# Attention scores from three terms instead of four, the low-part products of two heads in separate row halves of TensorE

## The chip, the cores and the metric

The kernel runs on one core of one Trainium2 chip. The metric is the device time of one execution in microseconds (us), the median of three runs. Engines are named as in the profile: PE is TensorE's matrix products, PEld its weight loads, DVE is VectorE, ACT is ScalarE, POOL is GpSimd, SPq is the queue of SyncE, which issues all DMAs.

## The reference

One residual block over 2048 rows of width 1024, float32. After an RMS norm, one projection gives q, k, v and the gates. Attention has four pairs of heads; each pair has two heads of 64 features for q and k, and one value head of 128 features. What matters here is one tile of 128 queries against the keys it may see:

```
sc = jnp.einsum('bqhd,bkhd->bhqk', qb, k) * scale        # two heads (h) of a pair, d = 64
sc = jnp.where(mask, sc, jnp.finfo(jnp.float32).min)     # chunk-causal
pr = jax.nn.softmax(sc, axis=-1).reshape(b, ATT_HEADS, 2, Q_BLOCK, s)
a  = pr[:, :, 0] - lam * pr[:, :, 1]
out = jnp.einsum('bhqk,bkhe->bqhe', a, v)
```

The rest (a short gated convolution, gates by sigmoid, two output projections, a norm) stands before and behind the attention.

## The kernel before

Float32 values are split in a high part of type fp32r and a low part, the rest. A product of two matrices is then a sum of products of parts: high by high, high by low, low by high (`split_product`, L936 to L939).

The stages in order: the norm and the v projection; the other projections (28 tiles of 128 features by 4 blocks of 512 rows, L973 to L980), whose q and k parts go to `qk_s` in memory; the attention stage; then for each block of 512 rows the two branch projections and `w_out`.

The attention stage has rounds R, one per tile of 128 queries (4 pairs by 16 tiles), laid out by the class `Plan`. In round R, PE computes the scores of tile R+1 (`score`, L987), turns the combined probabilities of tile R-1 with the identity (`turn`, L1003), and in every second round multiplies two tiles by the values (`values`, L1014). Keys come in chunks of up to 512. The positions are causal, so a tile has 1 to 4 chunks, its last one 128, 256, 384 or 512 wide. In all there are 160 chunks: 112 of 512 columns and 16 of each of the other three widths. Between these steps PE does the gate projections (`gates`, L1051, products at L1065), 1536 products of 512 columns that depend on nothing in the attention and fill its waits. `Plan` divides them over the rounds by comparing `tensor_columns` and `vector_columns`.

A chunk's scores are four products, two for each head. The key tile `k_sl` holds for each head the high part in partitions 0 to 63 and the low part in 64 to 127. The query tile `q_st` holds the same query part twice, in both halves of the partitions. So one product with 128 rows gives q_high by (k_high + k_low) (L999), and the other q_low by (k_high + k_low) (L1000): four terms in two products. The result lies in one of three banks, `bank[0]`, `bank[1]`, `bank[4]`, taken in turn. DVE then adds the mask, copies the scores to `e1` or `e2` and takes the maximum (`mask_max`, L1580, semaphore `scored`). A head's first product waits until the bank's last user is scored, three products back. After the last chunk DVE forms the bias (L1587, L1589), ACT the exponentials (L1267), DVE combines both heads (L1600), PE turns the result (L1010), ACT copies the high part (L1276), DVE the low part (L1616), and PE multiplies by the values (L1027).

SyncE issues `load_q` (L678, four DMAs for two tiles of queries), `load_k` (L662, two DMAs for 512 keys), `load_v` (L669), the gate weights `load_unit` (L685) and the stores, in one order.

Of the kernel before, what the change touches and what calls it, by code (L numbers as in the profile page):

```python
# [14 lines left out]
P = 128  # L15
# [58 lines left out]
UNITS = GATE_TILES * NB  # L74
PER_UNIT = 3 * KT
LEAD = 2 * PER_UNIT
K_IN, V_IN, Q_IN = 2 * 16, 2 * 16, 4 * 16
RING = 5

WO_AT = ((), (), (0,), (1,), (2,), (3,), (4, 5), (6, 7))  # L80
# [66 lines left out]
class Plan:  # L147
# [64 lines left out]
    def tensor_columns(self, R):  # L212
        n = 0
        if 0 <= R + 1 < TILES:
            n += 4 * self.keys(R + 1)
        if 0 <= R - 1 < TILES:
            n += 2 * self.keys(R - 1)
        if R % 2 == 0 and 2 <= R <= TILES:
            n += 6 * max(self.keys(R - 1), self.keys(R - 2))
        return n + 1200  # L220
# [32 lines left out]
def build(nc, t):  # L253

    with ExitStack() as whole:
# [3 lines left out]
        def held(name, shape, dt=F32, ctx=whole):  # L259
            return ctx.enter_context(nc.sbuf_tensor(name, shape, dt))  # L260
# [77 lines left out]


        kc = held("kc", [P, S], F32, room)  # L340
        q_st = [held(f"q_st{b}", [P, 2, 2, QB], F32R, room) for b in range(2)]
        k_sl = {i: held(f"k_sl{i}", [P, 2, BLK], F32R, room) for i in (3, 0, 1, 2)}
        sub = ExitStack()
        first_w = [held(f"first_w{i}", [P, 2, KT, P], F32R, sub) for i in range(2)]
# [191 lines left out]
        def _(sp):  # L536
# [121 lines left out]

            def load_k(plan, pair, c):
                i = plan.slot(pair * NT, c)  # L660
                for half in range(2):
                    sp.dma_start(k_sl[i][half * HD:(half + 1) * HD].bitcast(F32),  # L662
                                 qk_s[1, half, pair * P:(pair + 1) * P, c:c + BLK].rearrange("(h j) n -> j h n", h=2)
                                 ).then_inc(k_loaded[i], 16)

            def load_v(plan, pair, c):
                i = plan.slot(pair * NT, c)
# [5 lines left out]
            def load_q(plan, B):  # L673
                pair, ti = plan.tile(2 * B)
                qs = slice(ti // 2 * QB, ti // 2 * QB + QB)
                for half in range(2):
                    for at in (0, HD):
                        sp.dma_start(q_st[B % 2][at:at + HD, half].bitcast(F32),  # L678
                                     qk_s[0, half, pair * P:(pair + 1) * P, qs].rearrange("(h j) n -> j h n", h=2)
                                     ).then_inc(q_loaded[B % 2], 16)  # L680

            def load_unit(u):
                if u >= 4:
# [251 lines left out]
        def _(pe):  # L935
# [48 lines left out]
            score_bank = (0, 1, 4)  # L984

            def attend(plan):
                def score(G, c, wide, h):  # L987
                    ti = plan.tile(G)[1]
                    if h == 0 and plan.first_use(G, c):
                        pe.wait_ge(k_loaded[plan.slot(G, c)], (G // NT + 1) * K_IN)  # L990
                    if G % 2 == 0 and c == 0 and h == 0:
                        pe.wait_ge(q_loaded[G // 2 % 2], (G // 4 + 1) * Q_IN)
                    o = 2 * (plan.before(G) + c // BLK) + h
                    if o >= 3:
                        pe.wait_ge(scored, o - 2)
                    out = bank[score_bank[o % 3]][:, 0:wide]
                    k = k_sl[plan.slot(G, c)][:, h, 0:wide]
                    qs = slice(ti % 2 * P, ti % 2 * P + P)
                    nc.tensor.matmul(out, q_st[G // 2 % 2][:, 0, h, qs], k, start=True, stop=False)  # L999
                    nc.tensor.matmul(out, q_st[G // 2 % 2][:, 1, h, qs], k, start=False, stop=True  # L1000
                                     ).then_inc(qk_done, 1)

                def turn(G, c, wide):  # L1003
                    if c == 0:
                        pe.wait_ge(combined, G + 1)
                    o = plan.before(G) + c // BLK
                    if o >= 2:
                        pe.wait_ge(at_lo_done, o - 1)
                    for k in range(wide // P):
                        mm = nc.tensor.transpose(bank[5 + o % 2][:, k * P:(k + 1) * P],  # L1010
                                                 e1[G % 2][:, c + k * P:c + (k + 1) * P], ident[:])
                    mm.then_inc(turned, 1)

                def values(G, c, wide):  # L1014

                    B = G // 2
                    last = max(plan.keys(G - 1), plan.keys(G)) // P - 1
                    pe.wait_ge(at_lo_done, plan.before(G) + c // BLK + 1)
                    if plan.first_use(G, c) or plan.first_use(G - 1, c):
                        pe.wait_ge(v_loaded[plan.slot(G, c)], (G // NT + 1) * V_IN)  # L1020
                    if c == 0 and B:
                        pe.wait_ge(o_normed, B)

                    def step(k, x, start, stop):
                        q0 = P if plan.causal and k == last else 0
                        v = v_sl[plan.slot(G, k * P // BLK * BLK)][:, x // 2, k % QPB, :]
                        return nc.tensor.matmul(bank[7][:, q0:QB], v, (at_lo if x == 1 else at_hi)[:, k, q0:QB],  # L1027
                                                start=start, stop=stop)

                    if c == 0:  # L1030
                        step(0, 0, True, False)
                    for k in range(max(c // P, 1), (c + wide) // P):
                        for x in range(3):
                            step(k, x, False, False)
                    if (c + wide) // P - 1 == last:
                        step(0, 1, False, False)
                        step(0, 2, False, True).then_inc(pv_done, 1)

                def square_sums(B):
                    pe.wait_ge(sq_done, B + 1)  # L1040
                    if B:
                        pe.wait_ge(ln_done, B)
                    pe.wait_ge(es_ready, 2 * (B + 1))
                    nc.tensor.matmul(bank[7][:, QB:2 * QB], ones[:], o_sq[:], start=True, stop=False)
                    for i in range(2):
                        q0 = QB + plan.tile(2 * B + i)[1] % 2 * P
                        mm = nc.tensor.matmul(bank[7][:, q0:q0 + P], es[(2 * B + i) % 4][:], ident[:],
                                              start=False, stop=i == 1)
                    mm.then_inc(ss_done, 1)

                def gates(part):  # L1051
                    for x in range(part[0], part[1]):
                        u, i = divmod(x, PER_UNIT)
                        k, term = divmod(i, 3)
                        bb, g = divmod(u, GATE_TILES)
                        if i == 0:
                            if u < 2:
                                pe.wait_ge(first_in[u], 16)
                            else:
                                pe.wait_ge(unit_w[u % 2], 16 * (u // 2))  # L1060
                            if u >= 2:
                                pe.wait_ge(gate_out, u - 1)
                        if bb and g == 0 and term == 0 and k % 2 == 0:
                            pe.wait_ge(ht_in[k // 2], 32 * bb)
                        mm = nc.tensor.matmul(bank[2 + u % 2][:], unit_weights(u)[:, term // 2, k, :],  # L1065
                                              h_slot(bb, k)[:, term % 2, :], start=i == 0, stop=i == PER_UNIT - 1)
                        if i == PER_UNIT - 1:
                            mm.then_inc(unit_done, 1)
                        elif g == GATE_TILES - 1 and i == 5 and bb < NB - 1:
                            mm.then_inc(ht_free, 1)  # L1070


                pe.wait_ge(dve_done, done_at(LINE - 2, 3))
                gates((0, LEAD))
                pe.wait_ge(dve_done, done_at(LINE - 1, 0))
                for R in plan.rounds:
                    steps = plan.round(R)
                    for j, (turned_part, scored_part, value_part, part) in enumerate(steps):
                        if turned_part:
                            turn(R - 1, *turned_part)  # L1080
                        if scored_part:
                            for h in range(2):
                                score(R + 1, *scored_part, h)
                        if value_part:
                            values(R - 1, *value_part)
                        if R % 2 == 1 and 3 <= R <= TILES + 1 and j == min(1, len(steps) - 1):
                            square_sums((R - 3) // 2)
                        gates(part)
# [663 lines left out]
```

## Time and profile before

| | us |
|---|---|
| median of three runs | 1808.36 (1807.6 to 1809.15) |
| the profiled execution, its own time | 1808.52 |
| its span in the profile | 1806.7 |
| PE busy | 1758.4 (97%) |
| PEld busy | 1466.7 (81%) |
| DVE busy | 893.8 (49%) |
| ACT busy | 580.3 (32%) |
| DMA, mean rate | 182 GB/s |

Some 1.8 us lie outside the span. A product of 512 columns is shown as 390 ns long, but the next one starts about 227 ns after it: the shown length holds the time in the pipeline, so PE's busy share is a mark of where PE has work, and the distance from start to start is the cost of a product. Weight loads lie under the product before them. A row of the timeline gives start, length, engine, line, operation, tiles, sizes and how many instructions were merged, and in brackets idle time that the engine spent before it and what ended it.

### The profile page before, as it was taken

To read this page: it belongs to the slowest core of one execution; us is meant where nothing else is said; L and a number is where in the kernel's file an instruction comes from. 1 tells how busy PE (TensorE), PEld (TensorE's weight loads), DVE (VectorE), ACT (ScalarE), POOL (GpSimd) and SP (SyncE) were. 2 spreads that over 40 slices of the span, in tenths; PEclk is the share of its full clock that TensorE was granted. 3 is DMA by queue.
4 is the path that set the end of the run, shared out by engine and by line. 5 is a ranking of instruction groups with operands and counts; after the bars stand their busy time and mean duration, and the time that the engine had idled before them with its cause. 6 is when DMAs were issued, how large, how long until landed. Compare 5 with 4: busy or idle time off the path is not lost.

```text
span 1806.7 us, 22424 instructions
## 1 busy us (share of the span) xinstructions
PE 1758.4 (97%) x8512; PEld 1466.7 (81%) x8512; DVE 893.8 (49%) x1903; ACT 580.3 (32%) x1039; POOL 89.0 (5%) x74
## 2 busy tenths in 40 slices
PE   7999999999999999999999999999899889999998
PEld 6887888888888888788887888888788768888887
DVE  5547244445334511276666666766576344424242
ACT  5423112121101111245444544444444333313231
POOL 0000000000000000111101111111001000000000
PEclk9999999999999999999999999999999999999999
DMA  6557346465503546965674778556856775453532
GB/s 233 164 189 314 129 163 210 163 210 167 178 18 129 162 118 174 265 219 186 198 211 151 221 233 271 181 180 208 248 158 185 227 281 172 120 181 111 175 105 76
DMA packets 149574, 328.90 MB, mean 182 GB/s; under 512 B 14801, under 2 KB 68049, under 8 KB 135889
## 3 DMA queue, kind: packets, MB, share of 16 engines
q1 hardware_dynamic: 149458, 327.37, 57.3%
q8 instruction: 70, 1.15, 0.3%
q14 instruction: 46, 0.38, 0.1%
HBM read 216.16 MB, written 111.16 MB: 181 GB/s over the span
## 4 chain that ended last, share of the span: by engine, by line
PE 83%; DMA 7%; ACT 3%; SPq 3%; DVE 2%; issue 2%; DVEq 0%; ACTq 0%
PE bank L937 18%; PE bank L938 18%; PE bank L939 18%; PE bank L1065 15%; PE bank L1027 5%; PE bank L999 3%; PE bank L1000 3%; PE bank L1010 2%; DMA raw<-in_w_in 2%; DMA ring<-gate_s 2%; SPq L669 2%; ACT e L1267 2%; DMA w<-split_s 1%; DMA gate_s<-gate_st 1%; DVE at_lo L1616 1%
## 5 line engine op out<-in xcount | busy, mean ns | idle before, releaser
L937 PE MATMUL bank<-ht,w 128*128 128x512 f32 x896 | 349.9, 390 | 3.0 <-issue 3.0
L938 PE MATMUL bank<-ht,w 128*128 128x512 f32 x896 | 349.7, 390 | 0.0
L939 PE MATMUL bank<-ht,w 128*128 128x512 f32 x896 | 349.5, 390 | 0.0
L1065 PE MATMUL bank<-ht,w 128*128 128x512 f32 x912 | 238.8, 396 | 4.0 <-DMA w<-split_s 4.0
L937 PEld LDWEIGHTS bank<-ht,w 128*128 128x128 f32 x896 | 168.8, 188 | 38.7 <-issue 3.4
L939 PEld LDWEIGHTS bank<-ht,w 128*128 128x128 f32 x896 | 168.9, 188 | 35.2
L938 PEld LDWEIGHTS bank<-ht,w 128*128 128x128 f32 x896 | 168.9, 188 | 35.1
L1065 PEld LDWEIGHTS bank<-ht,w 128*128 128x128 f32 x912 | 167.2, 189 | 36.7 <-DMA w<-split_s 4.6
L1580 DVE CUSTOM_DVE_ANT_0 e<-bank,zeros 128x512 f32<-128x512 f32 x192 | 125.0, 688 | 131.0 <-PE bank L1000 130.5
L1267 ACT ACTIVATE e<-e,nbias 128x128 f32<-128x128 f32 (+15 forms) x128 | 152.8, 1197 | 74.7 <-DVE nbias L1589 74.6
L1065 PE MATMUL bank<-hx,w 128*128 128x512 f32 x576 | 157.2, 401 | 7.0 <-DMA w<-split_s 7.0
L1276 ACT ACTIVATE at_hi<-bank 128x512 fp32r<-128x512 f32 (+3 forms) x160 | 83.3, 528 | 172.3 <-PE bank L1010 172.2
L1027 PE MATMUL bank<-at_hi,v_sl 128*128 128x256 f32 (+1 forms) x576 | 118.0, 283 | 12.6 <-DVE at_lo L1616 12.4
L1065 PEld LDWEIGHTS bank<-hx,w 128*128 128x128 f32 x576 | 106.4, 192 | 28.4 <-DMA w<-split_s 8.6
L999 PE MATMUL bank<-k_sl,q_st 128*128 128x512 f32 (+3 forms) x320 | 128.3, 406 | 0.0
L926 POOL TENSOR_SCALAR mask<-kc,qc 128x128 f32<-128x128 f32 (+3 forms) x64 | 87.5, 1367 | 598.5 <-DVE mx L1580 598.0
L1000 PE MATMUL bank<-k_sl,q_st 128*128 128x512 f32 (+3 forms) x320 | 116.4, 368 | 0.0
L1027 PEld LDWEIGHTS bank<-at_hi,v_sl 128*128 128x128 f32 x576 | 95.1, 190 | 24.2 <-DVE at_lo L1616 21.9
L1616 DVE TENSOR_TENSOR at_lo<-bank,at_hi 128x512 fp32r<-128x512 f32 (+3 forms) x160 | 97.2, 608 | 32.5 <-ACT at_hi L1276 32.1
L937 PE MATMUL bank<-br,wa 128*128 128x512 f32 x256 | 101.1, 395 | 6.6 <-DVE ring L1664 5.9
L938 PE MATMUL bank<-br,wa 128*128 128x512 f32 x256 | 100.8, 394 | 0.0
L939 PE MATMUL bank<-br,wa 128*128 128x512 f32 x256 | 100.6, 393 | 0.0
(140 smaller groups left out, 2493.0 us busy)
## 6 DMA issues: line engine op xcount, KB each, us to landing
w<-split_s SPq DMA_DIRECT2D x62, 1024.0 KB, 5.4
split_s<-piece SPq DMA_DIRECT2D x24, 1024.0 KB, 5.0
q_st<-qk_s SPq DMA_DIRECT2D x128, 128.0 KB, 5.5
gate_s<-gate_st SPq DMA_DIRECT2D x64, 256.0 KB, 6.0
ring<-gate_s SPq DMA_DIRECT2D x64, 256.0 KB, 3.3
raw<-in_w_in SPq DMA_DIRECT2D x28, 512.0 KB, 5.7
ht_s<-ht SPq DMA_DIRECT2D x3, 4096.0 KB, 27.5
qk_s<-stage SPq DMA_DIRECT2D x48, 192.0 KB
```

The source lines that it names most:

```text
L926: nc.gpsimd.tensor_scalar(mask[m % 2][:, 0:wide], kc[:, c:c + wide], qc[:, plan.tile(G)[1]:plan.tile(G)[1] + 1], MASKED, ALU.is_gt, ALU.mu ...
L937: nc.tensor.matmul(out, left[0], right[0], start=start, stop=False)
L938: nc.tensor.matmul(out, left[0], right[1], start=False, stop=False)
L939: return nc.tensor.matmul(out, left[1], right[0], start=False, stop=stop)
L999: nc.tensor.matmul(out, q_st[G // 2 % 2][:, 0, h, qs], k, start=True, stop=False)
L1000: nc.tensor.matmul(out, q_st[G // 2 % 2][:, 1, h, qs], k, start=False, stop=True).then_inc(qk_done, 1)
L1027: return nc.tensor.matmul(bank[7][:, q0:QB], v, (at_lo if x == 1 else at_hi)[:, k, q0:QB], start=start, stop=stop)
L1065: mm = nc.tensor.matmul(bank[2 + u % 2][:], unit_weights(u)[:, term // 2, k, :], h_slot(bb, k)[:, term % 2, :], start=i == 0, stop=i == PE ...
L1267: nc.scalar.activation(e, e, ACT.Exp, bias=nbias[G % 2][:, h:h + 1], scale=SCALE, accum_out=esum[G % 2][:, h:h + 1]).then_inc(exp_done, 1)
L1276: nc.scalar.activation(at_hi[:, c // P:(c + wide) // P, q0:q0 + P], bank[5 + o % 2][:, 0:wide].rearrange("p (k n) -> p k n", n=P), ACT.Cop ...
L1580: nc.vector.tensor_tensor_reduce(e[:, c:c + wide], bank[(0, 1, 4)[o % 3]][:, 0:wide], mask[m % 2][:, 0:wide] if masked else zeros[:, 0:wid ...
L1616: nc.vector.tensor_tensor(at_lo[:, ks, q0:q0 + P], bank[5 + o % 2][:, 0:wide].rearrange("p (k n) -> p k n", n=P), at_hi[:, ks, q0:q0 + P]. ...
```

## The change

The low-by-low term is no longer computed. `q_st` now has three parts: the high part of head 0 and of head 1, each twice as before, and in the third part the low parts, head 0 in partitions 0 to 63 and head 1 in 64 to 127. In `k_sl` the halves of head 1 are exchanged: its high part lies in partitions 64 to 127. A chunk is then two products of 64 rows, q_low by k_high, head 0 in rows 0 to 63 and head 1 in rows 64 to 127 into two different banks, and then two products of 128 rows, q_high by (k_high + k_low), into the same two banks. There are still four products for each chunk, and four weight loads. All four stand behind one wait: both banks must be free, so the first product waits until the head of two products back is scored. `load_q` has three DMAs instead of four, `load_k` four of half the size instead of two. `Plan.tensor_columns` counts 3 columns for a key instead of 4. Below the change a line of the file stands 10 or 11 lines further down: L1009 and L1011 are the products of 64 and of 128 rows, and L1010, L1027, L1065 are L1021, L1038, L1076.

```
-            n += 4 * self.keys(R + 1)
+            n += 3 * self.keys(R + 1)
...
-        q_st = [held(f"q_st{b}", [P, 2, 2, QB], F32R, room) for b in range(2)]
+        q_st = [held(f"q_st{b}", [P, 3, QB], F32R, room) for b in range(2)]
+        held("q_fill", [P, 2, QB], F32, room)
...
             def load_k(plan, pair, c):
-                for half in range(2):
-                    sp.dma_start(k_sl[i][half * HD:(half + 1) * HD].bitcast(F32),
-                                 qk_s[1, half, pair * P:(pair + 1) * P, c:c + BLK].rearrange("(h j) n -> j h n", h=2)
+                for h in range(2):
+                    for half in range(2):
+                        r0 = (h + half) % 2 * HD
+                        sp.dma_start(k_sl[i][r0:r0 + HD, h].bitcast(F32),
+                                     qk_s[1, half, pair * P + h * HD:pair * P + (h + 1) * HD, c:c + BLK]
...
             def load_q(plan, B):
-                for half in range(2):
-                    for at in (0, HD):
-                        sp.dma_start(q_st[B % 2][at:at + HD, half].bitcast(F32),
-                                     qk_s[0, half, pair * P:(pair + 1) * P, qs].rearrange("(h j) n -> j h n", h=2)
+                for at in (0, HD):
+                    sp.dma_start(q_st[B % 2][at:at + HD, 0:2].bitcast(F32),
+                                 qk_s[0, 0, pair * P:(pair + 1) * P, qs].rearrange("(h j) n -> j h n", h=2)
+                sp.dma_start(q_st[B % 2][:, 2].bitcast(F32), qk_s[0, 1, pair * P:(pair + 1) * P, qs]
...
-                def score(G, c, wide, h):
+                def score(G, c, wide):
...
-                    o = 2 * (plan.before(G) + c // BLK) + h
-                    if o >= 3:
-                        pe.wait_ge(scored, o - 2)
-                    out = bank[score_bank[o % 3]][:, 0:wide]
-                    k = k_sl[plan.slot(G, c)][:, h, 0:wide]
+                    o = 2 * (plan.before(G) + c // BLK)
+                    if o >= 2:
+                        pe.wait_ge(scored, o - 1)
+                    out = [bank[score_bank[(o + h) % 3]][:, 0:wide] for h in range(2)]
+                    q, k = q_st[G // 2 % 2], k_sl[plan.slot(G, c)]
                     qs = slice(ti % 2 * P, ti % 2 * P + P)
-                    nc.tensor.matmul(out, q_st[G // 2 % 2][:, 0, h, qs], k, start=True, stop=False)
-                    nc.tensor.matmul(out, q_st[G // 2 % 2][:, 1, h, qs], k, start=False, stop=True
-                                     ).then_inc(qk_done, 1)
+                    for h in range(2):
+                        rows = slice(h * HD, (h + 1) * HD)
+                        nc.tensor.matmul(out[h], q[rows, 2, qs], k[rows, h, 0:wide], start=True, stop=False)
+                    for h in range(2):
+                        nc.tensor.matmul(out[h], q[:, h, qs], k[:, h, 0:wide], start=False, stop=True
+                                         ).then_inc(qk_done, 1)
```

The first piece of the order is PE's, in an early round of the first pair: four products with the identity, the scores of a chunk of 512 keys, and gate products behind them. This is how it stands before.

```order
3155 L1010 MATMUL bank6<-ident,e1_1 128x128 x4
3156 L999 MATMUL bank0<-k_sl0,q_st0 128x512
3157 L1000 MATMUL bank0<-k_sl0,q_st0 128x512
3158 L999 MATMUL bank1<-k_sl0,q_st0 128x512
3159 L1000 MATMUL bank1<-k_sl0,q_st0 128x512
3160 L1065 MATMUL bank2<-ht0,w0 128x512 x6
3161 L1065 MATMUL bank3<-ht0,w1 128x512 x2
```

The same place on PE in the changed kernel, where L1009 are the products with 64 rows:

```order
3155 L1021 MATMUL bank6<-ident,e1_1 128x128 x4
3156 L1009 MATMUL bank0<-k_sl0,q_st0 128x512
3157 L1009 MATMUL bank1<-k_sl0,q_st0 128x512
3158 L1011 MATMUL bank0<-k_sl0,q_st0 128x512
3159 L1011 MATMUL bank1<-k_sl0,q_st0 128x512
3160 L1076 MATMUL bank2<-ht0,w0 128x512 x6
3161 L1076 MATMUL bank3<-ht0,w1 128x512 x2
```

The number of products is the same; head 0's last product moved from the second place to the third, and the two heads' banks are now written alternately. The second piece is SyncE's, where the first keys of the attention are loaded, as it stands before.

```order
181 L685 DMA first_w<-split_s 128x2048
182 L669 DMA v_sl<-v_s 128x4x128 x2
183 L685 DMA first_w<-split_s 128x2048
184 L662 DMA k_sl<-qk_s 64x2x512 x6
185 L637 DMA qk_s<-stage 32x2x512
186 L637 DMA qk_s<-stage 48x2x512 x2
```

The same place on SyncE in the changed kernel:

```order
183 L689 DMA first_w<-split_s 128x2048
184 L672 DMA v_sl<-v_s 128x4x128 x2
185 L689 DMA first_w<-split_s 128x2048
186 L665 DMA k_sl<-qk_s 64x512 x12
187 L638 DMA qk_s<-stage 32x2x512
188 L638 DMA qk_s<-stage 48x2x512 x2
```

Three chunks of keys are now twelve issues of one head each instead of six of two heads; nothing else changed its place.

## Rows read from the trace of the kernel before

**Rows 1.** The page, part 1: busy time of each engine.
```profile
PE 1758.4 (97%) x8512; PEld 1466.7 (81%) x8512; DVE 893.8 (49%) x1903; ACT 580.3 (32%) x1039; POOL 89.0 (5%) x74
```
**Rows 2.** Windows, the attention stage: busy us, granted clock, DMA share, GB/s.
```profile
738.00:1430.00 692.00, 668.36 (x3693) 567.38 (x3692) 446.21 (x1275) 311.15 (x600) 85.64 (x62) 0.99 0.68 209
```
**Rows 3.** Waits, window 738 to 1430: us in total, times, longest.
```profile
DVE e L1580 <- PE bank L1000: 204.7, 122, 8.7
...
PEld bank L1027 <- DVE at_lo L1616: 21.7, 26, 2.7
...
PE bank L1027 <- DVE at_lo L1616: 12.4, 16, 2.2
PE bank L1065 <- DMA w<-split_s: 11.1, 5, 3.6
```
**Rows 4.** Timeline of PE, a chunk of 512 keys behind turns.
```profile
1108.79 0.60 PE L1010 MATMUL bank<-ident,e 128*128 128x128 f32 x4
1109.15 0.48 PE L999 MATMUL bank<-k_sl,q_st 128*128 128x512 f32 x1
1109.46 0.40 PE L1000 MATMUL bank<-k_sl,q_st 128*128 128x512 f32 x1
1109.70 0.40 PE L999 MATMUL bank<-k_sl,q_st 128*128 128x512 f32 x1
1109.93 0.40 PE L1000 MATMUL bank<-k_sl,q_st 128*128 128x512 f32 x1
1110.16 0.62 PE L1065 MATMUL bank<-hx,w 128*128 128x512 f32 x2
```
**Rows 5.** Timeline of PEld, the weight loads of the same chunk.
```profile
1109.12 0.19 PEld L999 LDWEIGHTS bank<-k_sl,q_st 128*128 128x128 f32 x1
1109.23 0.19 PEld L1000 LDWEIGHTS bank<-k_sl,q_st 128*128 128x128 f32 x1
1109.46 0.19 PEld L999 LDWEIGHTS bank<-k_sl,q_st 128*128 128x128 f32 x1
```
**Rows 6.** Timeline of PE, a chunk of 128 keys behind gate products.
```profile
1105.00 0.28 PE L1000 MATMUL bank<-k_sl,q_st 128*128 128x128 f32 x1
1105.11 0.27 PE L999 MATMUL bank<-k_sl,q_st 128*128 128x128 f32 x1
1105.22 0.27 PE L1000 MATMUL bank<-k_sl,q_st 128*128 128x128 f32 x1
```
**Rows 7.** Timeline of PE, a chunk of 384 keys behind a turn.
```profile
1120.10 0.34 PE L1000 MATMUL bank<-k_sl,q_st 128*128 128x384 f32 x1
1120.27 0.34 PE L999 MATMUL bank<-k_sl,q_st 128*128 128x384 f32 x1
```
**Rows 8.** The chain of waits before the longest stall of the values.
```profile
950.82 3.65 ACT e L1267 x4
954.47 0.30 ACT o_st L1298
954.77 0.50 ACT at_hi L1276
...
955.29 0.70 DVE at_lo L1616
...
956.04 1.64 PE bank L1027 x10
```
**Rows 9.** Timeline of DVE and then of PE, the tightest bank.
```profile
1050.01 0.69 DVE L1580 CUSTOM_DVE_ANT_0 e<-bank,zeros 128x512 f32<-128x512 f32 x1 [0.74 <-PE bank L1000]
...
1051.08 0.31 PE L999 MATMUL bank<-k_sl,q_st 128*128 128x128 f32 x1
```
**Rows 10.** Sources L662, L678: queue time of one issue in ns, min/median/max.
```profile
L662 SPq DMA_DIRECT2D k_sl<-qk_s x32: 573/608/1318, 705.8 to 1235.1; - x32
L678 SPq DMA_DIRECT2D q_st<-qk_s x128: 579/607/1772, 702.1 to 1398.5; - x128
```
**Rows 11.** Timeline of SPq, around the start of the attention.
```profile
719.03 4.47 SPq L662 DMA_DIRECT2D k_sl<-qk_s  x6
...
729.06 0.53 SPq L685 DMA_DIRECT2D w<-split_s  x1
...
755.73 0.43 SPq L803 DMA_DIRECT2D z_in<-z_s  x1
```

More of the change, by code:

```diff
@@ L76 @@
 LEAD = 2 * PER_UNIT
-K_IN, V_IN, Q_IN = 2 * 16, 2 * 16, 4 * 16
+K_IN, V_IN, Q_IN = 4 * 16, 2 * 16, 3 * 16
 RING = 5
@@ L660, in load_k @@
                 i = plan.slot(pair * NT, c)
-                for half in range(2):
-                    sp.dma_start(k_sl[i][half * HD:(half + 1) * HD].bitcast(F32),
-                                 qk_s[1, half, pair * P:(pair + 1) * P, c:c + BLK].rearrange("(h j) n -> j h n", h=2)
-                                 ).then_inc(k_loaded[i], 16)
+                for h in range(2):
[3 more added lines that the diff above has]
+                                     qk_s[1, half, pair * P + h * HD:pair * P + (h + 1) * HD, c:c + BLK]
+                                     ).then_inc(k_loaded[i], 16)
             def load_v(plan, pair, c):
@@ L675, in load_q @@
                 qs = slice(ti // 2 * QB, ti // 2 * QB + QB)
-                for half in range(2):
-                    for at in (0, HD):
-                        sp.dma_start(q_st[B % 2][at:at + HD, half].bitcast(F32),
-                                     qk_s[0, half, pair * P:(pair + 1) * P, qs].rearrange("(h j) n -> j h n", h=2)
-                                     ).then_inc(q_loaded[B % 2], 16)
+                for at in (0, HD):
+                    sp.dma_start(q_st[B % 2][at:at + HD, 0:2].bitcast(F32),
+                                 qk_s[0, 0, pair * P:(pair + 1) * P, qs].rearrange("(h j) n -> j h n", h=2)
+                                 ).then_inc(q_loaded[B % 2], 16)
+                sp.dma_start(q_st[B % 2][:, 2].bitcast(F32), qk_s[0, 1, pair * P:(pair + 1) * P, qs]
+                             ).then_inc(q_loaded[B % 2], 16)
             def load_unit(u):
@@ L986, in attend @@
             def attend(plan):
-                def score(G, c, wide, h):
+                def score(G, c, wide):
                     ti = plan.tile(G)[1]
-                    if h == 0 and plan.first_use(G, c):
+                    if plan.first_use(G, c):
                         pe.wait_ge(k_loaded[plan.slot(G, c)], (G // NT + 1) * K_IN)
-                    if G % 2 == 0 and c == 0 and h == 0:
+                    if G % 2 == 0 and c == 0:
                         pe.wait_ge(q_loaded[G // 2 % 2], (G // 4 + 1) * Q_IN)
-                    o = 2 * (plan.before(G) + c // BLK) + h
-                    if o >= 3:
-                        pe.wait_ge(scored, o - 2)
-                    out = bank[score_bank[o % 3]][:, 0:wide]
-                    k = k_sl[plan.slot(G, c)][:, h, 0:wide]
-                    qs = slice(ti % 2 * P, ti % 2 * P + P)
-                    nc.tensor.matmul(out, q_st[G // 2 % 2][:, 0, h, qs], k, start=True, stop=False)
-                    nc.tensor.matmul(out, q_st[G // 2 % 2][:, 1, h, qs], k, start=False, stop=True
-                                     ).then_inc(qk_done, 1)
+                    o = 2 * (plan.before(G) + c // BLK)
[3 more added lines that the diff above has]
+                    q, k = q_st[G // 2 % 2], k_sl[plan.slot(G, c)]
+                    qs = slice(ti % 2 * P, ti % 2 * P + P)
+                    for h in range(2):
[4 more added lines that the diff above has]
+                                         ).then_inc(qk_done, 1)
                 def turn(G, c, wide):
@@ L1081, in attend @@
                         if scored_part:
-                            for h in range(2):
-                                score(R + 1, *scored_part, h)
+                            score(R + 1, *scored_part)
                         if value_part:
```

## The prediction

> **What bounds the kernel now.** I read the page's first part first: PE has work for 97% of the span, DVE for half of it, ACT for a third [rows 1]. Then the windows view of the attention stage, the only stage that the change touches: in 692 us PE is busy for 668, DVE for 446, ACT for 311, at a granted clock of 0.99, which is the 2.4 GHz level [rows 2]. Then the waits of that stage, to see whether PE ever waits for the others: 12.4 us in 16 waits of the value products for `at_lo`, and 11.1 us in 5 waits for gate weights [rows 3]. DVE on its part waits 204.7 us for PE's scores. So PE sets the pace here, and a column saved on PE is time saved, except where a chain through DVE and ACT is late. Last the timelines of PE and PEld, for what one chunk of scores costs.
>
> **A chunk of 512 keys before.** From the first of four turns to the first gate product behind the scores it is 1110.16 - 1108.79 = 1.37 us [rows 4]. The products of the scores start 0.23 to 0.24 us apart (1109.46, 1109.70, 1109.93, 1110.16), mean 0.2325 us. Four of them are 0.93 us, which leaves 0.44 us for the four turns, 0.11 us each. A turn has 128 columns, a quarter of 512, but costs half as much as a 512-column product: its price is the next weight load. The two loads behind each other start at 1109.12 and 1109.23, 0.11 us apart, the third waits until 1109.46, when a product has started and freed the place [rows 5]. Products of 128 columns start 0.11 us apart too (1105.00, 1105.11, 1105.22) [rows 6]. So a weight load is 0.11 us of PEld's time, hidden under a product of 512 columns and not under one of 128.
>
> **The same chunk after.** Four weight loads and four products remain; the two of 64 rows lie in different row halves and write different banks, and I take them to run side by side. Behind the turns (the last turn's start as zero): weights of head 0 arrive at 0.11, of head 1 at 0.22; the low products run 0.11 to 0.34 and 0.22 to 0.455; the weights of the first full product are loaded from 0.22 on, under them; the full products end at 0.69 and 0.92. Before, four products end at 0.11 + 0.93 = 1.04. The gain is 0.12 us for each chunk behind turns: one product of 0.2325 goes, one weight load of 0.11 comes out from under cover, because the product behind which it hid was a turn. All 112 chunks of 512 keys follow turns of the same step in the plan: 112 x 0.12 = 13.4 us.
>
> The 16 chunks of 384 keys cost 0.17 to 0.18 us a product [rows 7], so 0.175 - 0.11 = 0.065 us is gained: 1.0 us. Of the 32 chunks of 256 and 128 keys, 18 stand behind turns, where four weight loads of 0.11 fill the chunk before and after: nothing. The other 14 stand behind gate products, under which both low weights hide; about one slot of 0.11 us goes: 1.5 us. Sum on PE: 13.4 + 1.0 + 1.5 = 15.9 us.
>
> No row shows a load of 64 rows. Bounds: 0.11 us as for 128 rows, or half, 0.055; the half would give 0.055 x 112 = 6 us more. I take 0.11, from the nearest row. The Trainium skill bears on this: "TensorE: Matmul & The Clock Gate", section on LDWEIGHTS, says that a load takes its time by columns and that fewer rows do not shorten it. By it the sum stays 15.9; by the other reading it would be 22.
>
> **What is given back.** At the 16 waits of the values for `at_lo` [rows 3], PE is not the bound. The chain before the longest runs from the exponentials over ACT's copy and DVE's difference to the value products [rows 8]; scores that PE finishes early there only lengthen the wait. Those 16 places give back 0.12 us each. Besides, head 0's last product now ends at 0.69 instead of 0.11 + 0.465 = 0.575 after the last turn, 0.11 us later, and DVE scores head 0 first; where DVE's chain is the bound, that is 0.11 us more. 16 x 0.23 = 3.7 us. (PEld counts 26 such waits, so 6 us is the upper end.) Elsewhere the later score costs nothing: DVE is idle before it, 204.7 us in all, and gate products cover PE.
>
> The new wait for two free banks: the first score of a chunk now needs head 0 of the chunk before to be scored. The tightest place in the trace has DVE's scoring start at 1050.01, end by 1050.70, and PE's next score at 1051.08 [rows 9], a margin of 0.38 us. The change moves PE 0.12 earlier and DVE 0.11 later, so 0.15 us is left: no wait. Behind it stand the value products and the gates, so if it did wait, all of PE would; the nine places whose margin is under 0.5 us would be 1 us at 0.1 us each.
>
> **DMAs.** `load_q` loses one issue in four, 32 times, and a quarter of its bytes; `load_k` doubles its issues from 32 to 64 at the same bytes. An issue of either is 0.61 us of the queue now [rows 10]; plain two-dimensional ones take 0.43 [rows 11]. Where the queue is in need, at the start of the stage, six key issues take 4.47 us ahead of the gate weights at 729.06 [rows 11], for which PE later waits. As twelve they take 5.2 us at 0.43 each, or 7.3 at 0.61: 0.7 to 2.8 us later, against two `load_q` that save 2 x (0.61 + 0.18) = 1.6 us ahead of it. Between -0.9 and +1.2; I take 0. The gate products keep their number, the plan only shifts one or two between rounds: 0.
>
> **Sum.** -15.9 + 3.7 = -12.2 us. The profiled execution took 1808.5 us (span 1806.7 and 1.8 around it), 0.2 above the median. So 1796 us. With the half-price load at one end (-18) and 6 us given back, 1 us of bank waits and 1.2 us of queue at the other (-7.7, and a little for what the sum leaves out), the forecast's own range is 1788 to 1803.
>
> **Rivals.**
> 1. *A switch between 64-row and 128-row products empties the array* (slower). Each chunk has two switches, from a turn or gate product to the pair and from the pair to the full products. The trace shows no such switch; every product has 128 rows. What a drain could cost is read from the overlap: a product of 512 columns is 0.40 us long and the next starts after 0.2325 [rows 4], so 0.17 us of it overlap. Two switches without overlap cost 0.33 us; against 0.12 gained, +0.21 us for each of 112 chunks is 23.5 us, for the 48 others (0.33 less 0.07 gained) 12.5, together +36: 1845 us. If the weight load of the full product waited for the drain too, 0.11 to 0.19 us more for 160 chunks: 1862 to 1875. It decides the sign once the two switches together cost over 0.08 us a chunk (12.2 / 160). For it: nothing in the trace excludes it. Against it: turns, float32 and fp32r products follow each other without a gap wider than a weight load. The Trainium skill says it outright: "TensorEngine Tiling (Array Packing)", section Key Properties, has changing the tiling mode drain TensorE, without a duration. By that rule the time is this rival's or the next one's; no run here shows it yet.
> 2. *A small switch cost*, a part of that overlap, some 0.05 us a chunk: 160 x 0.05 = 8 us of the 12.2 is gone, 1804 us.
> 3. *The two 64-row products run one after the other*, so the change does not do what it says. Then a chunk has four slots as before, 0 gained; head 0 is ready 0.23 us later at the 16 late places: +3.7, so 1808 to 1812 us. For it: two products never overlap in start in this trace. Against it: no two products here use different rows.
>
> **Chances.** Forecast 0.42; rival 2 0.16; rival 3, with other ways in which gain and loss cancel, 0.12; rival 1 0.30. A measurement of this kernel tells 0.2% (3.6 us) from no change. Faster: the forecast and most of rival 2, 0.55. Same: the rest of rival 2 and most of rival 3, 0.12. Slower: rival 1 and the rest, 0.33. The range runs from 1788, the end with cheap loads, to 1842, into rival 1, leaving out its upper half.
>
> **What would show it.** In the changed profile the two rows of L1009 start at most a weight load (0.11 us) apart, and under 0.02 us apart behind gates; 0.23 means rival 3. From the first turn to the gate product behind the scores it is 1.25 us instead of 1.37; 1.3 is rival 2, 1.5 or more rival 1, seen as a gap between the turns and L1009 and between L1009 and L1011. PE's busy time in the stage falls by some 12 us or its columns stand closer. The waits of L1038 for `at_lo` grow from 12.4 to some 16 us. No wait of L1009 for DVE's L1580 appears. The prediction is wrong if the pair is no shorter than two slots, if either switch costs over 0.05 us, or if the gate weights come late by more than 2 us over now.

## The result, and the profile after

The changed kernel takes 1825.78 us (1822.67 to 1827.17, 4 runs) against 1808.54 us before in the same comparison: 0.97% slower, ratio 1.0097, interval 1.0083 to 1.0111. The forecast was 1796 us. The profiled execution has a span of 1824.8 us, 18.1 more than before. Part 1 of its page, where the columns are busy time, share of the span and instructions:

```profile
PE 1782.4 (98%) x8512; PEld 1439.8 (79%) x8512; DVE 893.4 (49%) x1903; ACT 581.0 (32%) x1039; POOL 89.1 (5%) x74
```

Against [rows 1], PE is busy for 24 us more with the same 8512 products, its weight loads for 27 us less, and the other engines did not move. The windows view of the attention stage, to be laid beside [rows 2]:

```profile
738.00:1450.00 712.00, 694.54 (x3704) 543.23 (x3703) 445.45 (x1275) 311.65 (x601) 85.71 (x62) 1.00 0.63 198
```

PE has no work for 17 of 712 us, where it had none for 24 of 692. So the loss is no wait for another engine: the products themselves stand wider apart. The waits of that stage (us in total, times, longest):

```profile
DVE e L1590 <- PE bank L1011: 234.4, 128, 9.0
...
PEld bank L1011 <- issue: 30.3, 128, 0.3
PEld bank L1009 <- issue: 29.9, 156, 0.4
...
PE bank L1038 <- DVE at_lo L1626: 11.9, 13, 1.7
PE bank L1076 <- DMA w<-split_s: 5.2, 3, 2.5
...
PEld bank L1009 <- DVE mx L1590: 0.7, 4, 0.2
```

Two of these rows have no counterpart in [rows 3], the weight loads of the scores: PEld stands idle for 60 us ahead of them with no releaser ("issue"), 0.2 us each time. Below is the timeline of PE for one chunk of 512 keys, to be laid beside [rows 4]; rows of equal products are merged (x2, x4).

```profile
1118.51 0.60 PE L1021 MATMUL bank<-ident,e 128*128 128x128 f32 x4
1119.03 0.50 PE L1009 MATMUL bank<-k_sl,q_st 64*128 64x512 f32 x2
1119.46 0.73 PE L1011 MATMUL bank<-k_sl,q_st 128*128 128x512 f32 x2
1120.03 0.86 PE L1076 MATMUL bank<-hx,w 128*128 128x512 f32 x3
```

And PEld for the same chunk, beside [rows 5]:

```profile
1118.28 0.59 PEld L1021 LDWEIGHTS bank<-ident,e 128*128 128x128 f32 x4
1119.03 0.19 PEld L1009 LDWEIGHTS bank<-k_sl,q_st 64*128 64x128 f32 x2 [0.17 <-issue]
1119.46 0.30 PEld L1011 LDWEIGHTS bank<-k_sl,q_st 128*128 128x128 f32 x2 [0.24 <-issue]
1119.81 0.19 PEld L1076 LDWEIGHTS bank<-hx,w 128*128 128x128 f32 x1
```

The pair does run side by side: both products together are 0.50 us long, and both weight loads together 0.19 us. But when the row count changes, the next weights are not loaded ahead. In what follows such a change, from 128 to 64 rows or back, is called a switch, and a slot is the time from the start of one product to the start of the next. In [rows 4, 5] the load of L1000 starts at 1109.23, 0.23 us ahead of its product at 1109.46; here the pair's load starts at 1119.03, with the pair's own row, and the full product's at 1119.46, with its own row. From the first turn to the first gate product it is 1.52 us, where it was 1.37. By the starts it falls apart as 0.52 us from the first turn to the pair, 0.43 from the pair to the first full product, and 0.57 for the two full products, 0.11 more than two slots of 0.23. With the four turns put at 0.44 us as in the prediction, the two switches cost 0.08 + 0.20 + 0.11 = 0.39 us and save a slot of 0.23. (Run 4 below gives the same 0.39 without that division.)

Narrower chunks save a smaller slot at nearly the same price. Over both traces, take the time from the start of the last product ahead of a chunk to the start of the first one behind it, less that last product's own slot (0.11 us for a turn, 0.23 for a gate product). Its medians are 0.93 us before and 1.09 after for 512 keys, 0.70 and 0.92 for 384, 0.47 and 0.75 for 256, 0.39 and 0.62 for 128. With 112 chunks of the first kind and 16 of each other, PE is lengthened by 17.9 + 3.5 + 4.5 + 3.7 = 29.6 us. The span grew by 18.1. PE's idle time in the stage fell by 6.2 us (23.6 to 17.5), and the granted clock accounts for much of the rest. Four stretches before hold all its falls in the stage:

```profile
731.00:760.00 29.00, 24.98 (x105) 20.17 (x104) 8.01 (x33) 7.59 (x20) 4.31 (x3) 0.88 0.97 286
950.00:965.00 15.00, 12.77 (x74) 10.96 (x73) 9.49 (x25) 6.51 (x10) 0.43 (x1) 0.89 0.31 108
1285.00:1300.00 15.00, 10.54 (x50) 8.15 (x49) 7.42 (x24) 5.66 (x10) 2.00 (x1) 0.89 0.96 365
1420.00:1442.00 22.00, 19.20 (x91) 15.58 (x89) 4.85 (x16) 5.72 (x16) 0.00 (x0) 0.92 0.63 224
```

and after there is one, in the first of these two rows:

```profile
731.00:760.00 29.00, 26.50 (x115) 20.17 (x114) 9.42 (x39) 7.59 (x20) 5.46 (x4) 0.94 0.95 283
760.00:1450.00 690.00, 675.04 (x3621) 528.85 (x3620) 437.04 (x1239) 306.74 (x585) 80.25 (x58) 1.00 0.62 195
```

Each time the clock went to the lower of its two levels, 1.2 GHz, in a wait of PE or just behind it: before, three waits for gate weights (3.5, 3.6 and 2.8 us) and one for `at_lo` (2.2 us); after, one for gate weights (2.5 us). Not every such wait brings a fall: in run 1 below PE waits 2.9 us for gate weights once and the clock stays at 1.00 in the stage. What the clock gave back is 29 x 0.06 + 15 x 0.11 + 15 x 0.11 + 22 x 0.08 = 6.8 us, an upper estimate, since a part of the low stretches lay in the waits themselves. That leaves 29.6 - 6.2 - 6.8 = 16.6 us for a measured 18.1.

### The profile page after: what moved, and what is told of

The parts are those of the page before. It is cut to its first block, busy times and chain, and to the rows that moved or that the text cites. A ratio compares the mean times of both kernels' runs of the same rounds, so it can differ in the third digit from the quotient of the medians.

```text
span 1824.8 us, 22424 instructions
## 1 busy us (share of the span) xinstructions
PE 1782.4 (98%) x8512; PEld 1439.8 (79%) x8512; DVE 893.4 (49%) x1903; ACT 581.0 (32%) x1039; POOL 89.1 (5%) x74
## 4 chain that ended last, share of the span: by engine, by line
PE 84%; DMA 7%; ACT 3%; SPq 3%; DVE 2%; issue 2%; DVEq 0%; ACTq 0%
PE bank L941 17%; PE bank L942 17%; PE bank L943 17%; PE bank L1076 16%; PE bank L1038 6%; PE bank L1011 4%; PE bank L1009 3%; PE bank L1021 3%; DMA raw<-in_w_in 2%; DMA ring<-gate_s 2%; ACT e L1277 1%; DMA gate_s<-gate_st 1%; DMA w<-split_s 1%; PE bank L951 1%; SPq L672 1%
## 5 line engine op out<-in xcount | busy, mean ns | idle before, releaser
L1076 PE MATMUL bank<-ht,w 128*128 128x512 f32 x912 | 239.8, 396 | 2.5 <-DMA w<-split_s 2.5
L1076 PEld LDWEIGHTS bank<-ht,w 128*128 128x128 f32 x912 | 166.9, 189 | 34.9 <-DMA w<-split_s 2.9
L1076 PE MATMUL bank<-hx,w 128*128 128x512 f32 x576 | 153.5, 395 | 2.7 <-DMA w<-split_s 2.7
L1038 PE MATMUL bank<-at_hi,v_sl 128*128 128x256 f32 (+1 forms) x576 | 117.7, 283 | 12.2 <-DVE at_lo L1626 11.9
L1076 PEld LDWEIGHTS bank<-hx,w 128*128 128x128 f32 x576 | 104.7, 188 | 23.2 <-DMA w<-split_s 3.5
L1038 PEld LDWEIGHTS bank<-at_hi,v_sl 128*128 128x128 f32 x576 | 95.0, 190 | 23.0 <-DVE at_lo L1626 20.6
L1011 PE MATMUL bank<-k_sl,q_st 128*128 128x512 f32 (+3 forms) x320 | 107.0, 415 | 0.0
L941 PE MATMUL bank<-wo_hi,m_hi 128*128 128x512 f32 x256 | 100.0, 390 | 0.3 <-DVE wo_lo L1683 0.3
```

The costliest lines, as they stand in the source:

```text
L941: nc.tensor.matmul(out, left[0], right[0], start=start, stop=False)
L1011: nc.tensor.matmul(out[h], q[:, h, qs], k[:, h, 0:wide], start=False, stop=True).then_inc(qk_done, 1)
```

## The experiments

Theory S: the change of the row count is what costs. Rivals: W, the single wait for two banks, the later scores of head 0, the DMAs or the plan; P, the pair runs one after the other; Q, a pair is dear wherever it stands. All but run 11 are edits of the changed kernel's `score`, in which the original reads

```
for h in range(2):
    rows = slice(h * HD, (h + 1) * HD)
    nc.tensor.matmul(out[h], q[rows, 2, qs], k[rows, h, 0:wide], start=True, stop=False)
for h in range(2):
    nc.tensor.matmul(out[h], q[:, h, qs], k[:, h, 0:wide], start=False, stop=True).then_inc(qk_done, 1)
```

**1. The low products with 128 rows.**

```
-    rows = slice(h * HD, (h + 1) * HD)
-    nc.tensor.matmul(out[h], q[rows, 2, qs], k[rows, h, 0:wide], start=True, stop=False)
+    nc.tensor.matmul(out[h], q[:, 2, qs], k[:, h, 0:wide], start=True, stop=False)
```

> The changed kernel, but the two low products of a chunk have 128 rows: they take the whole third part of q_st and both halves of k_sl, so foreign low terms are added to the scores. Order, banks, waits, DMAs and plan stay as changed; no product has 64 rows. Theory S (each change between 64-row and 128-row products costs, because weights are not loaded ahead over it): no such change is left, so a chunk of 512 keys is back at 1.37 us from the first turn to the first gate product, and the time is that of the kernel before, 1805 to 1812 us. Rival W (the loss comes from the wait for two banks, from the later score of head 0, or from the DMAs and the plan): all these stay, so about 1825 us.

Measured: 1804.5 us, ratio to before 0.9994 (0.9981 to 1.0006). Its timeline of PE:

```profile
1111.21 0.60 PE L1020 MATMUL bank<-ident,e 128*128 128x128 f32 x4
1111.57 0.71 PE L1008 MATMUL bank<-k_sl,q_st 128*128 128x512 f32 x2
1112.12 0.62 PE L1010 MATMUL bank<-k_sl,q_st 128*128 128x512 f32 x2
1112.58 0.62 PE L1075 MATMUL bank<-ht,w 128*128 128x512 f32 x2
```

From the first turn to the first gate product it is 1.37 us again. The order, the wait, the DMAs and the plan of the change are all in it and together are not told from nothing. W falls; only the row count is left.

**2. One low product, of 64 rows.**

```
-for h in range(2):
-    rows = slice(h * HD, (h + 1) * HD)
-    nc.tensor.matmul(out[h], q[rows, 2, qs], k[rows, h, 0:wide], start=True, stop=False)
+nc.tensor.matmul(out[0], q[0:HD, 2, qs], k[0:HD, 0, 0:wide], start=True, stop=False)
```

Head 1's full product then starts its bank.

> The changed kernel without head 1's low product: one product of 64 rows in a chunk instead of two, the low term of head 1 is left out. Theory S: the pair runs side by side and its second member costs nothing, the two switches stay: 1822 to 1826 us. Rival P (the two 64-row products run one after the other, and that is the loss): a slot of 0.21 us less in 112 chunks, 1800 us or below.

Measured: 1823.18 us, ratio 1.0084 (1.0068 to 1.0101), not told from the changed kernel. The same chunk on PE:

```profile
1116.65 0.60 PE L1019 MATMUL bank<-ident,e 128*128 128x128 f32 x4
1117.18 0.50 PE L1007 MATMUL bank<-k_sl,q_st 64*128 64x512 f32 x1
1117.61 0.73 PE L1009 MATMUL bank<-k_sl,q_st 128*128 128x512 f32 x2
1118.18 1.53 PE L1074 MATMUL bank<-hx,w 128*128 128x512 f32 x6
```

One 64-row product takes the same 0.43 us as two. The second member of the pair is free; P falls.

**3. Both low products in the same rows.**

```
-    nc.tensor.matmul(out[h], q[rows, 2, qs], k[rows, h, 0:wide], start=True, stop=False)
+    nc.tensor.matmul(out[h], q[0:HD, 2, qs], k[0:HD, h, 0:wide], start=True, stop=False)
```

> The changed kernel with both low products in rows 0 to 63 (head 1 then takes head 0's low queries and its own low keys, so its low term is another one). Two switches in a chunk as in the changed kernel, but the two products cannot run side by side. Theory S: one slot of 0.21 us more in a chunk of 512 keys, 0.11 to 0.19 in the others, 31 us in all: some 1850 us, a little less where PE waits anyway. Rival P: they ran one after the other before too, so 1825 us.

Measured: 1852.85 us, ratio 1.0257 (1.024 to 1.0274). On PE, a chunk of 512 keys:

```profile
1118.99 0.73 PE L1008 MATMUL bank<-k_sl,q_st 64*128 64x512 f32 x2
1119.65 0.73 PE L1010 MATMUL bank<-k_sl,q_st 128*128 128x512 f32 x2
1120.22 1.55 PE L1075 MATMUL bank<-ht,w 128*128 128x512 f32 x6
```

The low products take 0.66 us where the pair takes 0.43: in the same rows they cost a slot more, as theory S says. Side by side is worth 27 to 30 us here (against the changed kernel's 1825.78 us, or against run 2, from the same comparison), and the change had that gain.

**4. Three full products.**

```
-for h in range(2):
-    rows = slice(h * HD, (h + 1) * HD)
-    nc.tensor.matmul(out[h], q[rows, 2, qs], k[rows, h, 0:wide], start=True, stop=False)
+nc.tensor.matmul(out[0], q[:, 2, qs], k[:, 0, 0:wide], start=True, stop=False)
```

> The changed kernel with one low product of 128 rows instead of the pair, for head 0 alone: three full products in a chunk, no 64-row product; head 1 has no low term and head 0 a foreign one. It is what the prediction hoped that the pair would cost. Theory S: a slot of 0.23 us less than before in a chunk of 512 keys, 0.11 to 0.17 in the others, 33 us, less what the waits of the value products and of the gate weights take back (up to 12 us): 1778 to 1790 us. If PE's products were not the bound of the stage (rival W): not below 1805 us.

As in run 2, head 1's full product starts its bank. Measured: 1787.04 us, ratio 0.9890 (0.9873 to 0.9906): 17.5 us less than run 1, not 32. First the chunk of 512 keys:

```profile
1113.76 0.60 PE L1019 MATMUL bank<-ident,e 128*128 128x128 f32 x4
1114.12 0.48 PE L1007 MATMUL bank<-k_sl,q_st 128*128 128x512 f32 x1
1114.43 0.63 PE L1009 MATMUL bank<-k_sl,q_st 128*128 128x512 f32 x2
1114.89 1.55 PE L1074 MATMUL bank<-ht,w 128*128 128x512 f32 x6
```

It takes 1.13 us, and the changed kernel's, with the pair in place of the one low product, 1.52: 0.39 us for two switches. The waits of PE in the attention stage show a part of what the time lacks. Run 1, four full products:

```profile
PE bank L1037 <- DVE at_lo L1625: 16.0, 16, 1.7
```

Run 4, three:

```profile
PE bank L1036 <- DVE at_lo L1624: 23.7, 22, 2.1
```

The value products wait 7.7 us longer for DVE. The granted clock shows most of the rest: over the executions of each run its median is 0.995 in run 1 and 0.992 in run 4, and 0.003 of 1787 us is some 5 us (an estimate). In run 4's trace it falls behind three of these very waits, as here behind one of 2.1 us:

```profile
850.00:865.00 15.00, 12.90 (x73) 11.26 (x72) 9.82 (x26) 5.23 (x9) 0.70 (x1) 0.89 0.31 99
```

So 7.7 + 5 of the missing 14.5 us are found.

**5. Three pairs.** The two full products become two more pairs; the place of the switches stays.

```
-for h in range(2):
-    rows = slice(h * HD, (h + 1) * HD)
-    nc.tensor.matmul(out[h], q[rows, 2, qs], k[rows, h, 0:wide], start=True, stop=False)
-for h in range(2):
-    nc.tensor.matmul(out[h], q[:, h, qs], k[:, h, 0:wide], start=False, stop=True).then_inc(qk_done, 1)
+for part in range(3):
+    for h in range(2):
+        rows = slice(h * HD, (h + 1) * HD)
+        mm = nc.tensor.matmul(out[h], q[rows, h if part else 2, qs], k[rows, h, 0:wide], start=part == 0, stop=part == 2)
+        if part == 2:
+            mm.then_inc(qk_done, 1)
```

> The changed kernel with the two full products replaced by two more pairs of 64 rows in the same row halves and banks (high by high, computed twice; the term high by low of the keys is left out). A chunk is then three pairs side by side, and the switches are again one in front and one behind. Theory S (the price is at the change of the row count only): the same as the changed kernel, 1818 to 1830 us. Rival Q (every pair costs 0.43 us from its own weight loads, wherever it stands): two pairs more at 0.2 us over a full slot in 160 chunks, 64 us less what the waits hide, so 1870 us or more.

Measured: 1826.8 us, ratio 1.0119 (1.0094 to 1.0143), as the changed kernel. On PE:

```profile
1117.61 0.96 PE L1010 MATMUL bank<-k_sl,q_st 64*128 64x512 f32 x6
1118.50 1.66 PE L1077 MATMUL bank<-hx,w 128*128 128x512 f32 x6
```

Six products of 64 rows take 0.89 us. The second pair starts at 1117.94 and the third at 1118.17, as the timeline shows from the second pair on and of the third alone:

```profile
1117.94 0.62 PE L1010 MATMUL bank<-k_sl,q_st 64*128 64x512 f32 x4
...
1118.17 0.39 PE L1010 MATMUL bank<-k_sl,q_st 64*128 64x512 f32 x2
```

From start to start that is 0.33, 0.23 and 0.33 us: between the second pair and the third it is one slot, and the distances next to a switch are 0.1 us longer. Q falls, and it is the change of kind that costs.

**6. Four switches in a chunk.** The two loops become one, so that each head has its low and then its full product.

```
 for h in range(2):
     rows = slice(h * HD, (h + 1) * HD)
     nc.tensor.matmul(out[h], q[rows, 2, qs], k[rows, h, 0:wide], start=True, stop=False)
-for h in range(2):
     nc.tensor.matmul(out[h], q[:, h, qs], k[:, h, 0:wide], start=False, stop=True).then_inc(qk_done, 1)
```

> The changed kernel in the order low of head 0, full of head 0, low of head 1, full of head 1: the same four products and terms, four switches instead of two, and no two 64-row products side by side. Theory S: against the run with both low products in the same rows (1852.9 us) two switches more; a pair of switches costs 0.15 us over before plus the slot of 0.23 us that it saved, 0.38 us, times 160 chunks 61 us: 1900 to 1915 us. If the switch were free and the loss elsewhere: 1855 us.

Measured: 1900.07 us, ratio 1.0520 (1.0496 to 1.0544), at the edge of the 1900 to 1915 expected. A chunk of 384 keys:

```profile
1108.95 0.44 PE L1009 MATMUL bank<-k_sl,q_st 64*128 64x384 f32 x1
1109.32 0.45 PE L1010 MATMUL bank<-k_sl,q_st 128*128 128x384 f32 x1
1109.69 0.43 PE L1009 MATMUL bank<-k_sl,q_st 64*128 64x384 f32 x1
1110.06 0.45 PE L1010 MATMUL bank<-k_sl,q_st 128*128 128x384 f32 x1
```

Products that start 0.17 us apart in [rows 7] start 0.37 us apart when each changes the kind: 0.2 us a switch. Against run 3 the two more switches of each chunk cost 47 us where the expectation took 61. The same medians as above give 60 us on PE; but PE's idle time in the whole span fell by 8 us (38.4 to 30.3), and the granted clock rose from 0.995 to 0.997 in the median, some 4 us by an estimate: again PE's added time was in part time that it had waited or spent at the lower clock.

**7. The pair behind the full products.** The two loops change places, and `start`, `stop` and the increments with them.

> The changed kernel with the pair behind the two full products: the same terms, two switches, one now between full scores and the pair, one between the pair and gate, value or sum products. Theory S: a switch costs the same wherever it is, 1820 to 1830 us. If the turns in front of the pair or the full products behind it were what made it dear (weights of a turn, both banks still in use), it would come near 1808 us.

Measured: 1826.85 us, ratio 1.0112 (1.0093 to 1.0131). The price does not hang on the place.

**8. Five full products.** Run 1 with one product more ahead of the last loop:

```
+nc.tensor.matmul(out[0], q[:, 1, qs], k[:, 0, 0:wide], start=False, stop=False)
```

> The full-row version (1804.5 us) with one more 128-row product in each chunk, head 1's high queries by head 0's keys added to head 0's scores: five full products, no 64-row product. It shows what PE time added to a chunk costs. One slot is 0.23 us in 112 chunks, 0.11 to 0.17 in 48, 33 us. With three products the time was 17 us less than with four, half of a slot's sum. If the other half is always taken up by waits: 1822 us. If waits only take back what PE saves, and PE is the bound once slower: 1835 us.

Measured: 1827.25 us, ratio 1.0109 (1.0090 to 1.0128). A slot more costs 22.8 us of the 32 us that its products last, nearer to the first case than to the second.

**9. Two full products.** The loop of the low products is left out.

> The changed kernel without any low product: the low term of the queries is left out for both heads, two full products in a chunk. With five, four and three full products the times were 1827.3, 1804.5 and 1787.0 us, steps of 22.8 and 17.5 us for 32 us of products each. If the waits of the value products grow as PE gets faster, the next step is smaller again: 10 to 16 us, 1771 to 1777 us. If a slot were worth the same everywhere: 1765 to 1768 us.

The full products then start their banks. Measured: 1771.09 us, ratio 0.9810 (0.9792 to 0.9827). Its wait of the value products:

```profile
PE bank L1035 <- DVE at_lo L1623: 34.3, 26, 3.1
```

With five, four, three and two products the times are 1827.3, 1804.5, 1787.0 and 1771.1 us, steps of 22.8, 17.5 and 15.9 us for 32 us of products each, and this wait is 10.2, 16.0, 23.7 and 34.3 us. The waits take back a part of what PE saves, more of it the faster PE gets. The clock does the same: its medians over the executions are 0.996, 0.995, 0.992 and 0.990, which is some 7, 9, 14 and 18 us of the time (an estimate, one less the clock times the time). The time, less this wait and less the clock's share, falls by some 30 us at each step. The four times come from three comparisons whose kernel before differs by up to 1.3 us, so a step is good to some 2 us.

**10. Switches in the wide chunks only.**

```
-    rows = slice(h * HD, (h + 1) * HD)
+    rows = slice(h * HD, (h + 1) * HD) if wide == BLK else slice(0, P)
```

> The changed kernel with 64-row low products in the 112 chunks of 512 keys only; in the 48 narrower chunks both low products have 128 rows and so add foreign low terms. Theory S: 48 chunks lose their two switches and gain nothing to lose, 0.22 to 0.28 us each on PE by the traces, 11 us; of the whole loss against the full-row version (21 us for 29 us on PE) that is its part, 8 us: 1816 to 1820 us. If the loss came once for a stage, a round or a DMA and not by the switch: 1825 us.

Measured: 1819.51 us, ratio 1.0075 (1.0060 to 1.0091), inside the 1816 to 1820 expected. But the kernel before was 2.6 us faster in this comparison; by the ratios (1.0097 and 1.0075) only some 4 us of the loss go without 48 of the 160 places, where 8 were expected, and the intervals overlap. Run 11, in the same comparison and with all its switches, took the same time. So this run agrees with a price at each switch and does not show it by itself.

**11. Another count in the plan.** `n += 5 * self.keys(R + 1)` instead of 3.

> The changed kernel, but Plan.tensor_columns counts 5 columns for a key instead of 3, about what a chunk now costs PE (1.08 us of 0.23 us slots for 512 keys); the gate products are shared out among the rounds by that. Theory S: the plan is not where the loss is, 1822 to 1828 us. If the wrong count in the plan made PE run dry in some rounds and DVE late in others: some 5 us faster or more.

Measured: 1819.44 us, ratio 1.0080 (1.0067 to 1.0094) against 1.0097 (1.0083 to 1.0111) for the changed kernel. This is under the expected 1822 to 1828, though not by the 5 us of the rival once the kernel before is counted, which was 2.6 us faster in this comparison too. Whether the plan is worth up to 0.2% stays open; it is not the loss.

## Why the prediction was wrong, step by step

- **What bounds the kernel: right.** PE sets the pace; DVE's and ACT's work did not move.
- **The pair side by side: right.** Both products in 0.50 us, and the second is free (run 2). The two weight loads also ran together in 0.19 us; the working had the second arrive 0.11 us behind the first. Both ends of its bounds for a 64-row load were beside the point.
- **The step that failed** is "the weights of the first full product are loaded from 0.22 on, under them", and before it that the pair's weights arrive under the turns. At either switch the load starts only with the product's own row, and 0.39 us in a chunk is paid for 0.23 saved. With it the sum on PE is +29.6 us instead of -15.9. The prediction's own sign for this, 1.5 us or more from the first turn to the gate product with gaps ahead of both kinds, is what the trace shows (1.52 us). Runs 1, 5 and 6 show that it is the change between 64 and 128 rows: none, 1804.5 us; two, with one pair or three between them, 1826 us; four, 1900 us.
- **The right answer stood among the rivals**, with 0.30, because no row of the trace before has a product with fewer than 128 rows, and the argument against it (unlike kinds follow each other closely) spoke of kinds with the same rows. The Trainium skill, "TensorEngine Tiling (Array Packing)", Key Properties, says that a change of the tiling mode drains TensorE. The runs agree that each change costs, 0.2 us either way with the late weight load included; how much of it is a drain and how much the load they do not separate. The rival's 0.33 us for two switches, read from the overlap of products, were near the measured 0.39. Its time, 1845 us, was too long for two reasons. It took 0.12 us as the pair's gain, a whole weight load less than the slot of 0.23 that the pair saved, so where it had +36 us on PE the traces have +29.6; and it gave nothing back, where the span grew by only 18.1. The stated range ran into this rival and so held the measured time, but the forecast had the wrong sign.
- **What is given back: too small.** It was put at 3.7 us for 16 waits of the value products. Taking 32 us of products out of the same kernel gave only 17.5 us (run 1 to run 4), so some 14 us is given back, of which the value products' wait shows 7.7 and the lower granted clock some 5. The prediction had no term for the clock. Had the switches been free, about half of 15.9 us would have been gained, by an estimate from that share.
- **The two banks: nearly right.** L1009 waits for DVE 0.7 us in 4 places; none was foretold.
- **DMAs and the plan: right at 0.** Run 1 has all of both and is at 0.9994. The wait for gate weights, 11.1 us before and 6.8 in run 1, is shorter in the profiles, but the times don't tell it. One size in the working was off: the twelve key issues, put at 5.2 to 7.3 us, took 9.26, and the next gate weights were issued at 730.71 instead of 729.06. The `v_sl` issues behind them took 12.06 us instead of 14.38, so the queue had caught up before the next gate weights (745.12 against 745.85), and no loss came of it.

```profile
716.72 9.26 SPq L665 DMA_DIRECT2D k_sl<-qk_s  x12
...
730.71 0.46 SPq L689 DMA_DIRECT2D w<-split_s  x1
```

No version with the terms of either kernel beat the kernel before. Runs 4 and 9 are faster, but by leaving low terms out. Two switches cost 0.39 us and one pair saves 0.23 in a chunk of 512 keys, so by an estimate from these figures a second pair between the same two switches would just turn it there (0.46 saved). The low products of two chunks at once would need four score banks where there are three; that was not tried.

## What to carry to other kernels

Count the changes of row count in TensorE's stream, not only its columns: here each way cost 0.2 us, nearly the worth of one product of 512 columns, and by these figures pairs side by side pay only if at least two of them stand between two changes. A way of using an engine that the trace of before never shows is the first thing to put a price and a large chance on. And a PE that is 97% busy is not a PE whose savings come through whole: here 50 to 70% did, since waits and the lower clock behind them took back the rest.

## What the runs showed of the hardware

- Two 64-row products in different row halves, each behind its own weight load, take the time of one (0.43 us against 0.43 with one alone), and their loads together 0.19 us.
- Six in a row, three pairs, take 0.89 us, and their starts are 0.23 us apart where no switch is next to them: among themselves they hide their weight loads (run 5).
- Two switches between 64 and 128 rows, one in and one out, cost 0.39 us around a pair of 512 columns (1.52 us against 1.13 in run 4), and one switch 0.2 us on a chunk of 384 keys with four of them (run 6). With the pair behind the full products the time is the same as ahead of them (run 7).
- The granted clock fell in or just behind waits of PE of 2.2 to 3.6 us in the attention stage before, and it fell more often the more PE waited: its medians are 0.996, 0.995, 0.992 and 0.990 with five, four, three and two full products (runs 8, 1, 4 and 9).
